# Gathering tokens from x itself in fp32, with eighteen weight slots and a reordered router gate's end

## What is computed

```python
x = x + _hier_moe(_rmsnorm(x, norm_ffn_g[i]), ...)     # 32 experts, 4 groups of 8; the best 2 of the best group
hp = _rmsnorm(x, norm_ple_g[i])
x = x + (p[i] @ w_ple[i]) * jax.nn.sigmoid(hp @ w_ple_gate[i])
...
return _rmsnorm(x, final_norm_g)

def expert(args):                                       # inside _hier_moe
    xb, e = args
    return (jax.nn.silu(xb @ w_g[e]) * (xb @ w_u[e])) @ w_d[e]
```

## Time and profile before

| | us |
|---|---|
| three runs | 1018.54, 1020.57, 1021.14 (median 1020.57) |
| the profiled execution | 1019.16 |
| its span in the profile | 1017.6 |
| PE busy | 955.7 (94%) |
| DVE busy | 636.0 (63%) |
| ACT busy | 536.8 (53%) |
| moved by DMA | 224.58 MB, mean 221 GB/s |

### The profile page before, as it was taken

The page is one execution under the profiler, slowest core; times in us unless marked ns, Lnnn a source line. Parts: engine busy times, 40 slices in busy tenths (PEclk is TensorE's granted clock), DMA queues, the critical chain, the costliest instruction groups (busy, mean ns, idle before and its releaser), DMA issues.

```text
span 1017.6 us, 14997 instructions
## 1 busy us (share of the span) xinstructions
PE 955.7 (94%) x5635; PEld 733.5 (72%) x5635; DVE 636.0 (63%) x1392; ACT 536.8 (53%) x976; POOL 84.2 (8%) x97
## 2 busy tenths in 40 slices
PE   6999899999999999999999999989899999887776
PEld 5777588888888877688888888768676655443345
DVE  3779768999846576769999846666785212110056
ACT  5757667666635565667666636765642111110055
POOL 0100001121100311001211101100000000000000
PEclk9999999999999999999999999999999999999979
DMA  8934346655565544356565563404759999999951
GB/s 270 383 128 125 103 126 197 196 168 204 204 190 186 181 151 125 93 165 199 167 199 201 178 193 124 151 21 167 278 219 370 403 418 419 421 422 421 421 201 42
DMA packets 99359, 224.58 MB, mean 221 GB/s; under 512 B 9535, under 2 KB 64210, under 8 KB 86994
## 3 DMA queue, kind: packets, MB, share of 16 engines
q1 hardware_dynamic: 99122, 223.04, 61.3%
q10 hardware_dynamic: 160, 0.53, 0.1%
HBM read 222.50 MB, written 1.05 MB: 220 GB/s over the span
## 4 chain that ended last, share of the span: by engine, by line
PE 76%; SPq 7%; DVE 6%; DMA 6%; ACT 3%; issue 2%; DVEq 0%; ACTq 0%
PE ps L560 72%; SPq L2971 6%; PE ps L564 3%; DMA ring<-in_w_ple_gate_dram 3%; DMA ringx<-in_w_up_e_dram 2%; DVE wl L1972 1%; DVE smb L1986 1%; DMA ring<-in_w_in_even_dram 1%; SPq L2974 1%; ACT wh L1428 0%; ACT hh L1425 0%; DVE pb L1977 0%; SPq L2956 0%; DVE hl L1982 0%; ACT pb L1425 0%
## 5 line engine op out<-in xcount | busy, mean ns | idle before, releaser
L1972 DVE TENSOR_TENSOR wl<-ring,wh 128x1024 fp32r<-128x1024 f32 (+3 forms) x212 | 269.0, 1270 | 107.1 <-ACT wh L1428 105.8
L1428 ACT ACTIVATE wh<-ring 128x1024 fp32r<-128x1024 f32 (+3 forms) x212 | 222.1, 1051 | 106.3 <-PE ps L560 101.2
L560 PE MATMUL ps<-hx,wh 128*128 128x512 f32 (+1 forms) x720 | 245.0, 389 | 0.1
L560 PE MATMUL ps<-hx,wl 128*128 128x256 f32 x704 | 194.6, 277 | 0.0
L560 PEld LDWEIGHTS ps<-hx,wh 128*128 128x128 f32 x720 | 134.0, 188 | 30.5 <-issue 0.6
L560 PEld LDWEIGHTS ps<-hx,wl 128*128 128x128 f32 x704 | 132.2, 188 | 0.0
L560 PE MATMUL ps<-wh,hh 128*128 128x512 f32 (+3 forms) x192 | 79.7, 415 | 3.2 <-DVE wl L1972 3.1
L2916 POOL TENSOR_TENSOR fs<-fs,rt 128x256 f32<-128x256 f32 x44 | 52.5, 1214 | 356.0 <-ACT fs L1425 356.0
L560 PE MATMUL ps<-ring,xg 128*32 128x256 f32 (+1 forms) x576 | 73.3, 381 | 7.8 <-DMA ring<-in_w_up_e_dram 5.7
L560 PE MATMUL ps<-wl,hh 128*128 128x512 f32 (+3 forms) x192 | 74.9, 390 | 0.0
L560 PE MATMUL ps<-wh,hl 128*128 128x512 f32 (+3 forms) x192 | 72.9, 387 | 0.0
(11 more groups left out here) (318 smaller groups left out, 1692.6 us busy)
## 6 DMA issues: line engine op xcount, KB each, us to landing
ring<-in_w_up_dram SPq DMA_DIRECT2D x88, 512.0 KB, 4.8
ring<-in_w_down_dram SPq DMA_DIRECT2D x22, 1024.0 KB, 5.1
ring<-in_w_up_e_dram SPq DMA_DIRECT2D x20, 1024.0 KB, 13.2
ring<-in_w_down_e_dram SPq DMA_DIRECT2D x18, 1024.0 KB, 20.9
ring<-in_w_gate_e_dram SPq DMA_DIRECT2D x16, 1024.0 KB, 13.4
ringx<-in_w_gate_e_dram SPq DMA_DIRECT2D x14, 1024.0 KB, 12.4
ring<-in_w_in_odd_dram SPq DMA_DIRECT2D x12, 1024.0 KB, 5.1
ringx<-in_w_down_e_dram SPq DMA_DIRECT2D x12, 1024.0 KB, 20.7
```

The costliest lines, as they stand in the source:

```text
L560: return e.matmul(o, l, r, start=start, stop=stop)
L1428: return e.activation(o, i, ACT.Copy)
L1972: return e.tensor_tensor(o, a, b, op)
```

## The change

- The ring of weights has eighteen slots: `NX` is 8 instead of 6. The room is that of `xh` and `xl`, which are gone, with `x_lo`.
- `gather` multiplies `S_` (now fp32) with x itself, read with a stride of 8 elements; for each 128 features and 128 tokens there is one fp32 product instead of two fp32r ones.
- `slot_rows` uses the fp32 weights `w3` (five columns) instead of `w10` (ten); `two_parts`, `wt10` and ACT's copy are gone, and DVE reads the bank.
- `route` has the router's 36 weight columns as the stationary operand and all 256 tokens as the moving one; ACT copies the 36 x 256 result to SBUF, and PE transposes it back in two pieces (`routeT`).
- The gate's end: ACT splits chunk 0 after the last `ysh`, then chunk 1, the others after `hhp`; DVE splits all low parts after `hlp`. PE's products for (0,0) and (1,0) are ordered by part (all hh x h, then all hl x h, then all hh x l); the finished order of outputs is (0,0), (1,0), (0,1), (1,1).

```diff
-NX = 6
+NX = 8
...
             b = take("route")
+            for k in range(8):
+                if k % 2 == 0:
+                    emptied(q, "nf2", k // 2)
+                w = mm(b[0:36, 0:S], ur[:, k, :], hT[:, k, :], k == 0, k == 7)
+            w.then_inc(of(full, "route"), 1)
+            b = take("routeT")
+            emptied(q, "route")
             for t in range(2):
-                for k in range(8):
-                    if t == 0 and k % 2 == 0:
-                        emptied(q, "nf2", k // 2)
-                    w = mm(b[:, t * 36:(t + 1) * 36], hT[:, k, t * P:(t + 1) * P], ur[:, k, :], k == 0, k == 7)
-            w.then_inc(of(full, "route"), 1)
+                w = tr(b[:, t * 36:(t + 1) * 36], at2[0:36, 0, t * P:(t + 1) * P])
+            w.then_inc(of(full, "routeT"), 1)
...
-                        for n_, (v, t) in enumerate(((xh, 0), (xh, 1), (xl, 0), (xl, 1))):
-                            w = mm(b[:, (k % 2) * S:(k % 2 + 1) * S], v[:, t, k * P:(k + 1) * P], S_[:, g % 2, t, :],
-                                   n_ == 0, n_ == 3)
+                        for t in range(2):
+                            w = mm(b[:, (k % 2) * S:(k % 2 + 1) * S], xk[:, t, :, k], S_[:, g % 2, t, :], t == 0, t == 1)
...
-                        w = mm(b2[:, 10 * j:10 * j + 10], slots_of(i, t), w10[:, t, i, :], t == 0, t == 1)
+                        w = mm(b2[:, 5 * j:5 * j + 5], slots_of(i, t), w3[:, t, i, :], t == 0, t == 1)
...
+            def gate_step(n, t, k, part):
+
+                c = 4 * n + k // 2
+                h, l = (v[:, k % 2 * 512:(k % 2 + 1) * 512] for v in gate_w[c])
+                if part == 2:
+                    q.wait_ge(w_split, c_gate[0] + c + 1)
+                elif part == 1:
+                    emptied(q, "np2", k // 2)
+                else:
+                    q.wait_ge(w_hi, c_gate[0] + c + 1)
+                    q.wait_ge(s_hh, hsplit["np2"] + k + 1)
+                v = (hhp, hlp, hhp)[part]
+                w = mm(bank[use[("gate", n), t][0]][:, :], v[:, k, t * P:(t + 1) * P], (h, h, l)[part],
+                       k + part == 0, k == 7 and part == 2)
+                if k == 7 and part == 2:
+                    w.then_inc(of(full, ("gate", n), t), 1)
+
             for t in range(2):
-                tk = slice(t * P, (t + 1) * P)
-                for n in range(2):
-                    b = claim(2 * t + n, ("gate", n), t)
-                    for k in range(8):
-                        c = 4 * n + k // 2
-                        q.wait_ge(w_split, c_gate[0] + c + 1)
-                        if t == 0 and n == 0:
-                            emptied(q, "np2", k // 2)
-                        wh_, wl_ = (v[:, k % 2 * 512:(k % 2 + 1) * 512] for v in gate_w[c])
-                        mm(b[:, :], hhp[:, k, tk], wh_, k == 0, False)
-                        mm(b[:, :], hhp[:, k, tk], wl_, False, False)
-                        w = mm(b[:, :], hlp[:, k, tk], wh_, False, k == 7)
-                    w.then_inc(of(full, ("gate", n), t), 1)
+                claim(2 * t, ("gate", 0), t)
+            for part, t, k in product(range(3), range(2), range(8)):
+                gate_step(0, t, k, part)
+            for t in range(2):
+                claim(2 * t + 1, ("gate", 1), t)
+                for part, k in product(range(3), range(8)):
+                    gate_step(1, t, k, part)
...
         def scalar(e):
...
-            for n in range(2):
-                emptied(q, (2, "out"), 0, n)
-                copy(xhk[:, 0, 64 * n:64 * n + 64], xk[:, 0, 64 * n:64 * n + 64]).then_inc(s_xhi, 1)
...
-            copy(xhk[:, 1], xk[:, 1]).then_inc(s_xhi, 1)
+            evac(at2[0:36, 0, :], "route", rows=36, cols=S)
...
-                b = filled(q, "wsl", g)
-                if g >= 2:
-                    q.wait_ge(s_wsl, g - 1)
-                copy(wt10[:, g % 2, :, :].rearrange("p j c -> p (j c)"), b[:, 0:20]).then_inc(of(drained, "wsl", g), 1)
...
-                if i == 9:
-                    for c in range(3):
-                        gate_hi(c)
...
+            gate_hi(0)
             warm()
+            gate_hi(1)
             general(e, "ACT")
...
-            for c in range(3, 8):
+            for c in range(2, 8):
                 gate_hi(c)
...
-            for t, n in ((0, 0), (0, 1), (1, 0)):
+            for t, n in ((0, 0), (1, 0), (0, 1)):
                 sigmoid(t, n)
-            q.wait_ge(s_sgm, 2)
+            q.wait_ge(s_sgm, 3)
...
         def vector(e):
...
-                own.inc(tt(rsl[:, 2 * g:2 * g + 2], v[:, :, 4], v[:, :, 9], ALU.add))
-                for h in range(len(members[2 * g])):
-                    w = tt(wsl[r * h:r * h + r, 2 * g:2 * g + 2], v[r * h:r * h + r, :, h], v[r * h:r * h + r, :, 5 + h], ALU.add)
+                v, r = filled(q, "wsl", g)[:, 0:10].rearrange("p (j c) -> p j c", c=5), P // len(members[2 * g])
+                for h in range(len(members[2 * g])):
+                    cp(wsl[r * h:r * h + r, 2 * g:2 * g + 2], v[r * h:r * h + r, :, h])
+                cp(rsl[:, 2 * g:2 * g + 2], v[:, :, 4]).then_inc(of(drained, "wsl", g), 1)
...
-            for c in range(3, 8):
+            for c in range(8):
                 gate_lo(c)
...
-            for t, n in ((0, 0), (0, 1), (1, 0)):
+            for t, n in ((0, 0), (1, 0), (0, 1)):
                 gated(t, n)
```

More of the change, by code:

```diff
@@ L192, in build @@
         wroom.close()
[L193 to L197, removed]
+        r1, S_, ScT, xg, ringx, ysh, ysl, smr, wsl, rsl = opened(
+            ("S_", [P, 2, 2, S], F32), ("ScT", [P, 4, S], F32R), ("xg", [P, 2, 8, S], F32), ("ringx", [P, NX, UW], F32),
+            ("ysh", [P, DM], F32R), ("ysl", [P, DM], F32R),
+            ("smb", [P, 3, 384], F32), ("wsl", [P, 16], F32), ("rsl", [P, 16], F32))
         hT = xg[:, 1, :, :]
         r1.close()
-        r1, gfl, _, gw2, gw3, hhp, hlp, sg, gw0 = opened(
+        r1, gfl, _, gw2, gw3, hhp, hlp, gw0, sg = opened(
             ("gfl", [P, DM], F32), ("gap0", [P, DM], F32), ("gw2", [P, 2, 1024], F32R), ("gw3", [P, 10, 1024], F32R), *HH,
-            ("sg", [P, 2, 1024], F32), ("gw0", [P, 4, 1024], F32R))
+            ("gw0", [P, 4, 1024], F32R), ("sg", [P, 2, 1024], F32))
         r1.close()
@@ L1384, in tensor @@
             for part in range(2):
-                q.wait_ge(s_xlo, 3 + part)
                 gather(0, part)
@@ L1910, in scalar @@
                     emptied(q, "gu", i - 2)
[L1911 removed]
+                emptied(q, "wsl", i // 2)
                 act(fs[:, i % 2, :], b[:, 0:S], ACT.Silu, scale=rsl[:, i:i + 1]).then_inc(s_msil, 1)
@@ L2642, in bc @@
                 return v.unsqueeze(2).to_broadcast([P, 2, n])
-            def x_lo(t, h):
-                q.wait_ge(s_xhi, 2 + t)
-                ks = slice(4 * h * P, 4 * (h + 1) * P)
-                tt(xl[:, t, ks].rearrange("q (k p) -> q p k", p=P), xk[:, t, :, 4 * h:4 * h + 4],
-                   xh[:, t, ks].rearrange("q (k p) -> q p k", p=P).bitcast(F32), ALU.subtract).then_inc(s_xlo, 1)
             q.wait_ge(s_sq, SQ["nf2"])
             ts(st[:, 8:10], st[:, 0:2], 1.0 / DM, EPS, ALU.mult, ALU.add).then_inc(s_var, 1)
-            x_lo(0, 0)
             q.wait_ge(s_std, RV["nf2"])
             rcp(rin[:, 12:14], st[:, 16:18]).then_inc(s_rstd, 1)
-            x_lo(0, 1)
             q.wait_ge(s_rstd, RV["nf2"])
-            b = filled(q, "route")
+            b = filled(q, "routeT")
             for t in range(2):
                 w = stt(rl_[:, t, 0:36], b[:, 36 * t:36 * t + 36], rinv_of("nf2", t), brt[:, :], ALU.mult, ALU.add)
-            w.then_inc(of(drained, "route"), 1)
-            emptied(q, "route")
+            w.then_inc(of(drained, "routeT"), 1)
+            emptied(q, "routeT")
             lgr = rl_[:, :, 32:36]
@@ L2737, in of_both @@
                 return tt(o, x_, y_, ALU.add)
-            def two_parts(i0, i1):
-                g = w10[:, :, i0:i1, :]
-                own.inc(cp(g[:, :, :, 0:5], w3[:, :, i0:i1, :]))
-                tt(g[:, :, :, 5:10], w3[:, :, i0:i1, :], g[:, :, :, 0:5].bitcast(F32), ALU.subtract).then_inc(s_wt, 1)
             def gate_lo(c):
@@ L2784, in vector @@
             own.inc(cp(w3[:, :, :, 4], rin[:, 12:14].unsqueeze(2).to_broadcast([P, 2, 10])))
-            own.inc(cp(w3[:, :, 0:3, 0:2], wt[:, :, 0:6].rearrange("p t (i c) -> p t i c", c=2)))
-            two_parts(0, 3)
+            cp(w3[:, :, 0:3, 0:2], wt[:, :, 0:6].rearrange("p t (i c) -> p t i c", c=2)).then_inc(s_wt, 1)
+            q.wait_ge(s_wt, 1)
             own.inc(of_both(keyp[:, :, NS:8], 0, 2, k12))
@@ L2789, in vector @@
             slot_rows(0)
-            own.inc(of_both(w3[:, :, 3, 0:2], 0, 2, w12))
-            two_parts(3, 4)
+            of_both(w3[:, :, 3, 0:2], 0, 2, w12).then_inc(s_wt, 1)
             for i in range(10):
@@ L2800, in vector @@
                     ask(e, "DVE")
-                if i == 9:
-                    for c in range(3):
-                        gate_lo(c)
```

(3 more changed lines are left out.)

12 lines of the change are left out of this document (3 added, 9 removed).

## The result

| | before | after |
|---|---|---|
| median | 1018.78 us (5 runs, 1017.87 to 1021.14) | 1029.45 us (5 runs, 1026.21 to 1030.07) |
| span of the profiled execution | 1017.6 | 1028.4 (time 1030.07) |

The ratio is 1.0088 with a 95% interval of 1.0074 to 1.0103: slower by about 9 us. The forecast was +2.7 us, or 1023.3 with a range to 1028. That was too low: the changed kernel's median lies 1.5 above the range. (The gate at the end, called the router gate in the title and in the prediction, is `w_ple_gate`; the router of the experts is another product.)

A forecast was written before the change was run, and what follows sets the result against it. PE sets the pace early in the MoE, until `down(3)`; then the weight stream does. Stream end +5.3, MoE end -6.9, gate products +1.7, clock +1.7, tail +0.9 sum to +2.7 us: median 1023.3, range 1018.5 to 1028.

The forecast's parts named there:

- X: What PE loses up to the end of `down(3)`, from router, gathers and slot weights together: 10.9 us.
- Router, +0.8: Before `embed`, PE waits for ACT's copy of the router result and transposes it back: 0.8 us later.
- gather(0) +2.9 and half gathers +5.8: Up to `down(3)`, fp32 products make gather(0) 2.9 us longer and the four half gathers after it 5.8 together.
- The strided stationary: Gather's weight load reading every eighth fp32 of x: taken as 0, at twice the load +1.5 us.
- Bare load: Rival: the gather's strided weight loads no longer overlap the products, 11 us more, 1034 us; chance 0.12.
- Slot weights, +1.35: `slot_rows`: four short products become eight fp32 instructions, +0.45 us, three times up to `down(3)`.
- Eighteen slots: Weight ring: two more units land early, worth up to -5.0 us; with PE's lag the stream's end (L) moves +5.3.
- faster: Rival: PE's lag stays below the slots' lead, so they give all of 5.0 us; 1013.0 us, chance 0.14.
- End of the MoE, -6.9: From the end of the last down (T) to ACT's first `hh` (H): 5.6 us instead of 12.5.
- Gate products, +1.7: After ACT's first `hh`, PE waits for later chunks, so the gate products end 25.7 us after it, not 24.0.
- clock, +1.7: Sparse first gate products lower PE's granted clock: 3.4 us at half speed; a rival without the drop had chance 0.22.
- Tail, +0.9: After the gate products, the new output order delays ACT's `Square`, and the last sigmoid slips by 0.9 us.

The follow-up runs named there:

- e1: The changed kernel with the gather's stationary operand read as 128 neighbouring columns of x instead of every eighth one; ratio to before 1.0059.
- e4: The changed kernel with sixteen ring slots instead of eighteen, the other tiles kept in place; ratio to before 1.0132.
- e10: The changed kernel with the router of before (32 products, no copy and no transposes back); ratio to before 1.0081.
- e12: The changed kernel with the router of before and a mended end (products by halves of k, outputs reordered, last two gate units held); ratio to before 1.0026.
- e5: The kernel before with the changed gate end alone; router, gather and sixteen slots stay; ratio to before 1.0014.
- e7: The kernel before with the changed end, mended: products by halves of k, outputs (0,0), (0,1), (1,0), (1,1), last two gate units held; ratio to before 0.9957.
- e9: As e7, but ACT squares both row blocks of x for np2; ratio to before 0.9956.
- e2: The changed kernel without PE's general path, its code and its branch after the last scatter; ratio to before 1.0046.

## Where the prediction was wrong and where right, point by point

- **What bounds the kernel:** right. PE's lag up to `down(3)` less two units of stream gives the end of the stream: 13.6 - 5.0 = 8.6, and T moved by 8.6; in e1 it is 11.0 - 5.0 = 6.0 and 6.1. With sixteen slots (e4) T moved by 15.1 at an X of 13.6, so the rule is good to some 1.5 us and the exact agreement is in part chance.
- **Router, +0.8:** 0.75 by its rows. Another 0.4 us lies ahead of gather(0) (it starts 1.2 later, not 0.8). It goes with the fp32 gather and not with the router: from the start of the last `embed` to gather(0) it is 1.80 us in after and also in e10 and e12, which have the old router, and 1.40 in before, e5, e7 and e9. No term had it. Contiguous columns (e1) don't take it away.
- **gather(0) +2.9 and half gathers +5.8:** 3.4 and 7.8 (4.02 to 4.06 us each). This is the first failed step, "The strided stationary ... I take 0". It costs 0.027 an instruction, 2.6 us by e1. The prediction's upper bound was 1.5. The rows of DVE that I scaled from are 1.07 and 0.70 us for the same size, which is 1.5 times; the 1.7 per element has no source in them. Either gave a load still covered by the product. The load's own row is 1.8 times longer, and it shows although product and load overlap: a half gather takes 4.02 us for its 16 instructions in after and 3.55 in e1, 0.25 and 0.22 each. With contiguous columns X is 11.0, against 10.9 in the sum. "Bare load" (+11) was far too high.
- **Slot weights, +1.35:** right. `slot_rows` takes 0.45 more than before, three times.
- **Eighteen slots:** the price of two units, 5.0, fits e4's 4.5 (ratio) and 6.5 (profile). The sum took 5.3 for L, between two readings that differ only because one uses 2.49 us a unit where the prediction's own division (143.1 / 57) gives 2.51; with 2.51 both give 5.9, and X less two units was the reading that held. The rival "faster" needed X below 5.0; X was 13.6. Eighteen slots without the fp32 gather weren't run, since their room is that of `xh` and `xl`; that alone they would gain 5.0 is not shown.
- **End of the MoE, -6.9:** the second failed step: "its branch and the 16 transposes T + 5.3". The transposes' start slipped by the stop of 5.1, and the stretch gave -2.1. e2 gives 5.4 for T to H against 5.6 predicted, so the working for ACT's side holds. In before the gap was 0.65 and stood in the trace; I took it as the branch's price. It was what was left of the fetch with the stream running out and eight slow scatter products to cover it. With fewer chunks split ahead of `ysh`, the branch came while the stream was still full, and with 1.2 us of products behind the last wait.
- **Gate products, +1.7 and clock, +1.7:** 25.7 (+1.7) in five other runs with this end and +3.3 in the profiled execution after, where the clock fell a second time. So one of six executions with this end shows the clock's 1.7, and that the stretch agrees with the forecast (+3.3 for +3.4) is in part luck. In all six the clock was already low from the stop when the first products began, which the prediction did not know of. Its mechanism, a fall behind the sparse start alone, is seen in e2.
- **Tail, +0.9:** +0.8.

Adding up: 3.3 too little up to T, 4.8 at the stop, 0.3 from the start, and 0.2 too much behind H make 8.2; 2.7 + 8.2 = 10.9, the span grew by 10.8. The profiled execution is the slowest of the five. With the gate stretch of 25.7 that the other five runs show, its growth would be 9.2, near the 9 of the ratio.

## What to carry to other kernels

A branch over a large block costs the fetch of code behind it, counted from the engine's last wait ahead of it; here 3.5 us with the DMA engines nearly idle and 6.3 beside a full stream, less the work that lies between. So before moving work across a branch, look at which stream runs there and at what covers the fetch; a short gap in the old trace isn't its price. A stationary operand in SBUF may skip every other fp32 element for nearly nothing, but at every fourth the load takes 1.7 times as long, and it shows even under products of 256 columns. Where a stream sets the end, price a lag by the last wait that holds the stream back, and let the trace's units of stream convert slots into time. (All figures are of this kernel.)

## What the runs showed of the hardware that I had not expected

- PE stood 5.1 us at a branch with a full weight stream, 2.2 to 2.7 us with the DMA engines idle, 0.65 us in before, where most of the fetch lay under the scatter, and none without the branch. In all thirteen profiled executions with the branch PE went on 1.44 to 1.48 us after a packet of the instruction queue had landed.
- A weight load of 128 x 128 fp32 takes 190, 196, 332 and 336 ns at strides of 1, 2, 4 and 8 elements.
- The granted clock fell to 0.50 beside or just behind thirty-two short fp32 products in both profiled executions with this router and eighteen slots, and in none of four with sixteen. The cause stays open.
